# Two groups of a projection made together with seven block products for eight, and the groups' order changed

## The reference, cut to what matters

```python
z = rmsnorm(x, norm_g) @ w_in            # (256, 2048) @ (2048, 6144)
q_a, k_a, v_a, g_a, u_p, g_p, q_m, g_m = split(z)   # 1024 x4, 512 x4
y_a = causal_attention(q_a, k_a, v_a) * silu(g_a)   # 8 heads of 128, one block
y_p = windows_pool(u_p, w_pool, pool_scale) * silu(g_p)
mk, mv = split(rmsnorm(mem, mem_norm_g) @ w_mem_kv)  # 256 memory tokens
y_m = softmax(q_m @ mk.T) @ mv * silu(g_m)          # 4 heads of 128
out = rmsnorm(x + concat(y_a, y_p, y_m) @ w_out, final_norm_g)
```

## Time and profile before

| | |
|---|---|
| median of 3 runs | 434.19 us (433.77 to 434.23) |
| profiled execution | 435.72 us, span 433.9 us |
| TensorE busy | 424.4 us |
| VectorE busy | 285.3 us |
| ScalarE busy | 232.1 us |
| GpSimd busy | 36.0 us |
| read from HBM | 90.72 MB, 214 GB/s over the span |

### The profile page before, as it was taken

One profiled execution on the slowest core, in us unless ns is written; L12 is line 12 of the kernel. 1 busy time (PEld: TensorE's weight loads), 2 busy tenths in 40 slices (PEclk: granted clock), 3 DMA queues, 4 the chain that ended last, 5 costly groups with the idle time before them and its releaser, 6 DMA issues.

```text
span 433.9 us, 5989 instructions
## 1 busy us (share of the span) xinstructions
PE 424.4 (98%) x2256; PEld 364.9 (84%) x2256; DVE 285.3 (66%) x308; ACT 232.1 (53%) x314; POOL 36.0 (8%) x60
## 2 busy tenths in 40 slices
PE   9999999999999999999999999999999999999993
PEld 8888888878888888888888888888899888888882
DVE  4875764265484657646558686967677479897842
ACT  6764684284343434646554544555465566765621
POOL 1000000000100000000023140002000211000160
PEclk9999999999999999999999999999999999999998
DMA  8999969969856565443635655474745999567023
GB/s 283 401 402 412 406 203 351 115 223 124 313 186 201 174 211 168 148 144 97 210 106 170 203 186 193 152 237 147 239 150 187 252 403 256 210 233 284 18 84 111
DMA packets 27387, 93.20 MB, mean 215 GB/s; under 512 B 3680, under 2 KB 4192, under 8 KB 26464
## 3 DMA queue, kind: packets, MB, share of 16 engines
q1 hardware_dynamic: 24336, 82.21, 58.0%
q10 hardware_dynamic: 2448, 8.52, 5.1%
q0 software_dynamic: 576, 2.10, 2.8%
HBM read 90.72 MB, written 2.10 MB: 214 GB/s over the span
## 4 chain that ended last, share of the span: by engine, by line
PE 91%; DMA 3%; issue 2%; DVE 1%; ACT 0%; POOL 0%; DVEq 0%; POOLq 0%; ACTq 0%
PE ps L521 33%; PE ps L524 16%; PE ps L537 8%; PE ps L539 8%; PE ps L538 8%; DMA rstd_rows<-rstd_in 3%; PE ps L502 3%; PE ps L574 2%; PE ps L573 2%; PE ps L575 2%; PE ps L558 1%; PE ps L559 1%; PE ps L557 1%; PE ps L509 1%; PE ps L655 1%
## 5 line engine op out<-in xcount | busy, mean ns | idle before, releaser
L967 DVE TENSOR_TENSOR w_lo<-w_raw,w_hi 128x1024 fp32r<-128x1024 f32 x135 | 170.3, 1276 | 96.1 <-ACT w_hi L746 95.9
L521 PE MATMUL ps<-xT,w_hi 128*128 128x512 f32 x640 | 201.7, 396 | 1.0 <-DVE w_lo L967 1.0
L746 ACT ACTIVATE w_hi<-w_raw 128x1024 fp32r<-128x1024 f32 x135 | 141.0, 1057 | 109.7 <-PE ps L524 59.8
L524 PEld LDWEIGHTS ps<-xT,w_lo 128*128 128x128 f32 x640 | 120.2, 188 | 28.4
L524 PE MATMUL ps<-xT,w_lo 128*128 128x256 f32 x640 | 125.8, 278 | 0.0
L521 PEld LDWEIGHTS ps<-xT,w_hi 128*128 128x128 f32 x640 | 97.8, 189 | 1.4 <-DVE w_lo L967 1.2
L537 PE MATMUL ps<-w_hi,xT 128*128 128x512 f32 x64 | 25.3, 396 | 0.0
L539 PE MATMUL ps<-w_hi,xT 128*128 128x512 f32 x64 | 24.9, 390 | 0.0
L538 PE MATMUL ps<-w_lo,xT 128*128 128x512 f32 x64 | 24.9, 389 | 0.0
L847 ACT ACTIVATE part_b<-ps 128x1024 f32<-128x1024 f32 x11 | 11.3, 1028 | 19.8 <-PE ps L524 19.8
L537 PE MATMUL ps<-w_hi,yT 128*128 128x512 f32 x46 | 17.9, 389 | 0.0
(11 more groups left out here) (178 smaller groups left out, 539.1 us busy)
## 6 DMA issues: line engine op xcount, KB each, us to landing
w_raw<-in_w_in SPq DMA_DIRECT2D x96, 512.0 KB, 4.3
w_raw<-in_w_out SPq DMA_DIRECT2D x30, 512.0 KB, 5.1
w_raw<-in_w_mem_kv SPq DMA_DIRECT2D x13, 512.0 KB, 12.8
x_t_raw<-in_x_t SPq DMA_DIRECT2D x8, 256.0 KB, 13.5
rows<-in_x ACTq DMA_DIRECT2D x2, 1024.0 KB, 10.5
rows<-in_mem ACTq DMA_DIRECT2D x2, 1024.0 KB, 13.1
f<-in_w_out SPq DMA_DIRECT2D x4, 512.0 KB, 7.8
f<-in_w_out POOLq DMA_DIRECT2D x4, 512.0 KB, 9.4
```

Of the source, the lines that this page charges most:

```text
L521: pe.matmul(ps[:, bank0(g) + f, :], hi[:, t, f * P:(f + 1) * P], moving[:, kt], start=(kt == 0), stop=(kt == KT - 1), skip_group_check=True)
L524: m = pe.matmul(ps[:, bank0(g) + f, 0:S], lo[:, t, f * P:(f + 1) * P], moving[:, kt, 0], start=False, stop=(kt == KT - 1), skip_group_chec ...
L746: act.activation(halves_of(n)[0], whole_of(n), ACT.Copy).then_inc(hi_done, 1)
L967: dve.tensor_tensor(lo, whole_of(n), hi.bitcast(F32), ALU.subtract).then_inc(lo_done, 1)
```

## The change

V0 and V1 are made together as OUT1 and OUT2 are: 22 units, of which 14 are block products with 6 matmuls each, and 8 plain units. The sums of blocks of x are made by VectorE in K0 (`x_sum`) and split (`xs_hi`, `xs_lo`); the sums of weights come from a transfer that adds, on GpSimd's queue behind `mkT`, and from VectorE (`weight_sum`). ScalarE copies four finished products, scaled, into `v` and `gate`; `values_one` and `values_two` complete the values. U comes next, with job 0, then GA0 with job 1, GA1, GP. The squares of mem, its reciprocal root, its write and its read come two units later. The gate GA1 is now followed by GP.

```diff
-(MK, MV, Q0, Q1, K0, K1, V0, V1, GA0, GA1, U, GP, QM, GM, OUT0) = range(15)
+(MK, MV, Q0, Q1, K0, K1, V0, V1, U, GA0, GA1, GP, QM, GM, OUT0) = range(15)
...
+BLOCKS = 2
+
+
+def pair_units(one, two):
+    return ((N5, 0), (M2, 0), (N5, 1), (M2, 1), (one, 4), (M3, 0), (one, 5), (M1, 0), (M3, 1), (one, 6), (M1, 1),
+            (M6, 0), (one, 7), (M4, 0), (M4, 1), (M6, 1), (two, 4), (N7, 0), (two, 5), (two, 6), (N7, 1), (two, 7))
+
+
+def pair_loads(one, two):
+    return ((M2, 0), (M2, 1), (one, 4), (M3, 0), (one, 5), (M3, 1), (M6, 0), (M6, 1), (one, 6), (one, 7),
+            (two, 4), (two, 5), (two, 6), (two, 7))
...
+PAIRS = ((V0, V1), (OUT1, OUT2))
+V_UNITS, PAIR_UNITS = pair_units(V0, V1), pair_units(OUT1, OUT2)
+V_LOADS = pair_loads(V0, V1)
+LOADS = pair_loads(OUT1, OUT2) + tuple((LAST, a) for a in range(PPG))
+EXTRA = len(V_UNITS) - 2 * PPG
+FEWER = 2 * PPG - len(V_LOADS)
+V_PAIR = V0 * PPG
+V_END = V_PAIR + len(V_UNITS)
...
+SUM_STEPS = {V_PAIR - 2: (0, F6, 0), V_PAIR + 4: (0, F6, 1), V_PAIR + 6: (0, F7, 0), V_PAIR + 9: (0, F7, 1),
+             PAIR + 2: (1, F6, 0), PAIR + 4: (1, F6, 1), PAIR + 6: (1, F7, 0), PAIR + 9: (1, F7, 1)}
...
+X_SUM_STEPS = {K0 * PPG + 2: 0, K0 * PPG + 3: 1, K0 * PPG + 4: 2, K0 * PPG + 5: 3}
+BANK = {V0: 0, V1: 2, OUT0: 4, OUT1: 0, OUT2: 2, LAST: 4}
 TOKENS_ON_ROWS = (MV, V0, V1)
-CAUSAL_JOBS = {V1: 0, GA0: 1}
+CAUSAL_JOBS = {U: 0, GA0: 1}
 MEM_JOB = GM
-JOBS = (V1, GA0, GM)
+JOBS = (U, GA0, GM)
 FACTOR = {Q0: SCALE, Q1: SCALE, QM: SCALE, GA0: 0.5, GA1: 0.5, GP: 0.5, GM: 0.5}
-BRANCHES = (V1, GA0, GP, GM)
-SQUARE_STEPS = {16: (0,), 17: (1,), 18: (2,), 19: (3,), 24: (4,), 25: (5,), 26: (6,), 27: (7,)}
+BRANCHES = (U, GA0, GP, GM)
+SQUARE_STEPS = {16: (0,), 17: (1,), 18: (2,), 19: (3,), 26: (4,), 27: (5,), 28: (6,), 29: (7,)}
...
+X_MEAN, MEM_MEAN = 20, 32
+SPREAD_WRITE, SPREAD_READ = {22: 0, 34: 1}, {24: 0, 36: 1}
...
+                if a == 1:
+                    sp.wait_ge(x_lo, PPG)
+                    for i in range(BLOCKS):
+                        sp.dma_start(x_f4[:, i], in_dram[V1 - Q0, 2 * i]).then_inc(f4_landed[0][i], 16)
+                if a == 5:
+                    for i in range(BLOCKS):
+                        sp.dma_start(x_f567[:, i, 0], in_dram[V0 - Q0, 2 * i]).then_inc(f5_landed[0][i], 16)
+                sp.wait_ge(lo_done, K0 * PPG + a + 1)
+                load(K1 * PPG + a, in_dram, K1 - Q0, a)
+            for r, (g, a) in enumerate(V_LOADS):
+                if r < RAW:
+                    sp.wait_ge(lo_done, K1 * PPG + r + 1)
+                else:
+                    slot_free(0, *V_LOADS[r - RAW])
+                pair_load(0, V_PAIR + r, in_dram, Q0, g, a)
...
+            for k in range(BLOCKS):
+                pool.wait_ge(f4_landed[0][k], 16)
+                pool.dma_start(x_f4[:, k], in_dram[V0 - Q0, 2 * k], accum_op=ALU.add).then_inc(f4_summed[0][k], 16)
+            for k in range(BLOCKS):
+                pool.wait_ge(f5_landed[0][k], 16)
+                pool.dma_start(x_f567[:, k, 0], in_dram[V0 - Q0, 2 * k + 1], accum_op=ALU.add).then_inc(f5_summed[0][k], 16)
...
+                if g == GA0:
+                    pool.wait_ge(pv_done, 4)
+                    for buf in (u_pad, sum_a, sum_b):
+                        pool.memset(buf[:, :, 0:PAD], 0.0).then_inc(pads_zero, 1)
...
+            def unit_of_pair(n):
+
+                q = pair_of(n)
+                g, a = unit(n)
+                if n == BEGIN[q]:
+                    pe.wait_ge(s_split, q + 1)
+                if (g, a) == (M1, 0):
+                    pe.wait_ge(snapped, snaps_done(q, SNAPS[M2, 1]))
+                if (g, a) == (PAIRS[q][0], 4):
+                    pe.wait_ge(snapped, snaps_done(q, SNAPS[N5, 1]))
+                if (g, a) == (M4, 0):
+                    pe.wait_ge(snapped, snaps_done(q, SNAPS[M1, 1]))
+                if (g, a) == (PAIRS[q][1], 4):
+                    pe.wait_ge(snapped, snaps_done(q, SNAPS[M4, 1]))
+                pe.wait_ge(lo_done, n + 1)
+                (pair_piece if g < GROUPS else block_product)(n).then_inc(piece_used, 1)
...
+                if V_PAIR <= n < V_END:
+                    if unit(n) in SNAPS:
+                        bank = bank0(V0) if g == N5 else bank0(V1) + 1
+                        h = int(g in (N5, M4))
+                        dst = {M2: v[:, 0, COLS:], N5: v[:, 1, 0:COLS], M1: v[:, 0, 0:COLS],
+                               M4: gate[:, 0:TPP, :].rearrange("p f s -> p (f s)")}[g]
+                        act.wait_ge(piece_used, n + 1)
+                        act.activation(dst, ps[:, bank, :], ACT.Copy, scale=rstd_in[:, 0, h:h + 1]).then_inc(snapped, 1)
+                    for m in pieces_to_split(n):
+                        split_hi(m)
+                    continue
...
+                if n == K0 * PPG + 6:
+                    act.wait_ge(x_summed, 1)
+                    act.activation(xs_hi[:, :, :, :, :], s_raw[:, :, :, :, :], ACT.Copy).then_inc(s_hi_done, 1)
...
+            def x_sum(j):
+
+                def part(s, k, h):
+                    return xT[:, 0:BLOCKS * NF, k, h * P:(h + 1) * P].bitcast(F32).rearrange(
+                        "p (i s t) c -> p i s t c", i=BLOCKS, s=2)[:, :, s]
+
+                dst = s_raw[:, :, j]
+                low = gate[:, 0:NF, :].rearrange("p (i t) (a c) -> p i t a c", i=BLOCKS, a=2)[:, :, :, 0]
+                if j == 0 or j == 2:
+                    left, right = ((0, 1), (1, 1)) if j == 0 else ((0, 0), (0, 1))
+                    dve.tensor_tensor(low, part(left[0], 1, left[1]), part(right[0], 1, right[1]), ALU.subtract)
+                    settle(dve.tensor_tensor(dst, part(left[0], 0, left[1]), part(right[0], 0, right[1]), ALU.subtract))
+                    settle(dve.tensor_tensor(dst, dst, low, ALU.add))
+                else:
+                    before, s, op = (s_raw[:, :, 0], 0, ALU.subtract) if j == 1 else (s_raw[:, :, 1], 1, ALU.add)
+                    settle(dve.tensor_tensor(dst, before, part(s, 0, 0), op))
+                    m = dve.tensor_tensor(dst, dst, part(s, 1, 0), op)
+                    if j == 1:
+                        settle(m)
+                    else:
+                        m.then_inc(x_summed, 1)
+
+            def split_sums(lo, hi):
+
+                dve.tensor_tensor(lo[:, :, :, :, :], s_raw[:, :, :, :, :], hi[:, :, :, :, :].bitcast(F32),
+                                  ALU.subtract).then_inc(s_split, 1)
+
+            def values_one():
+
+                first = slice(0, COLS)
+                dve.wait_ge(rstd_ready, 1)
+                dve.wait_ge(snapped, snaps_done(0, SNAPS[M4, 1]))
+                settle(dve.tensor_tensor(v[:, 1, first], v[:, 1, first],
+                                         gate[:, 0:TPP, :].rearrange("p f s -> p (f s)"), ALU.subtract))
+                dve.wait_ge(piece_used, unit_in(0, M6, 1) + 1)
+                for h, op in ((0, ALU.subtract), (1, ALU.add)):
+                    m = dve.scalar_tensor_tensor(out=v[:, h, first], in0=ps[:, bank0(V0) + h, :], scalar=rstd_in[:, 0, h:h + 1],
+                                                 in1=v[:, h, first], op0=ALU.mult, op1=op)
+                m.then_inc(evacuated, 1)
...
+            def values_two():
+
+                second = slice(COLS, 2 * COLS)
+                dve.wait_ge(piece_used, V_END)
+                dve.scalar_tensor_tensor(out=v[:, 0, second], in0=ps[:, bank0(V1), :], scalar=rstd_in[:, 0, 0:1],
+                                         in1=v[:, 0, second], op0=ALU.mult, op1=ALU.add)
+                dve.tensor_scalar(v[:, 1, second], ps[:, bank0(V1) + 1, :], rstd_in[:, 0, 1:2], None, ALU.mult
+                                  ).then_inc(evacuated, 1)
...
-                if g in TOKENS_ON_ROWS:
-                    dst = {V0: v[:, :, 0:COLS], V1: v[:, :, COLS:]}[g]
-                    dve.wait_ge(rstd_ready, 1)
-                    for h in range(TH):
-                        m = dve.tensor_scalar(dst[:, h], ps[:, bank0(g) + h, :], rstd_in[:, 0, h:h + 1], None, ALU.mult)
-                    m.then_inc(evacuated, 1)
-                    return
...
+                if g == U:
+                    m.then_inc(evacuated, 1)
+                    dve.wait_ge(evacuated, U + 1)
+                    dve.wait_ge(rstd_spread[0], 16)
+                    dve.tensor_tensor(dst[:, :, :], dst[:, :, :], x_rstd[:, :, :].to_broadcast([P, NF, S]), ALU.mult
+                                      ).then_inc(u_ready, 1)
+                    return
...
+                    for m in pieces_to_split(n):
+                        split_lo(m)
+                    if n in SUM_STEPS:
+                        weight_sum(*SUM_STEPS[n])
+                    if n == V_PAIR + 16:
+                        values_one()
+                    if n == V_END - 1:
+                        values_two()
+                    continue
...
-                if g == V0 and a == 4:
+                if g == GA1 and a == 5:
...
```

(47 more changed lines are left out.)

191 lines of the change are left out of this document (99 added, 92 removed).

## The result

The changed kernel takes 441.28 us (median of 6 runs, 439.81 to 443.7) against 434.08 (6 runs, 433.75 to 434.23): ratio 1.0171, interval 1.0138 to 1.0203. It is slower by 7.2 us. The sign was forecast, the size was not: 438.6 is 2.7 too low, and the time is 0.1 above the range's upper end of 441.2. Its runs also spread over 3.9 us where those of before spread over 0.5.

What follows compares the result with a forecast made beforehand. TensorE's list was taken to bound the kernel, busy 424.4 of 433.9 us. Terms -2.3 + 0.6 + 0.9 + 1.1 + 0.6 + 3.5 = +4.4 us gave 438.6 us, range 435.2 to 441.2.

Steps and rivals of the forecast that it cites:

- gain of the seven products: V0 and V1 made as a pair: 180 matmuls on TensorE instead of 192, saving 2.3 us.
- K0 and K1: x_sum, later reciprocal roots and VectorE's lock with GpSimd delay unit 43's w_lo: +0.6 us, between 0 and 3.
- start of the pair: After K1's end, unit 51's w_lo stands behind kT, wanted at 145.8 and coming at 146.67: +0.9 us.
- job 0 in U: Scores after U's first unit wait for V1's values, which stand behind a split: +1.1 us.
- job 1's turning in GA0: U's evacuation on VectorE delays the mask, so the second pair of probabilities comes late: +0.6 us.
- GP: GA1's gate falls into GP with the pool windows; unit 5's w_lo 2.2 us late, unit 7's 1.2: +3.5 us.
- Hidden: Work costing no time: extra splits, four sums, product copies, 3 MB more of weights, mv moved to GA1.
- Rival B: First sum late through adding transfers issued after mkT, delaying unit 51: 440.6 us, up to 442; chance 0.13.
- A fall of the clock behind a hole: Lower granted clock after TensorE's holes would make the forecast wrong; the earlier 0.97 us hole brought none.
- The shift from the profiled execution to the median, -1.5: Profiled execution forecast at 440.1 us; median of runs taken 1.5 lower, giving 438.6.
- C: Rival: one split more of lead on VectorE everywhere, holes summing to less than 2.3 us: 433.0 us; chance 0.10.
- D: Rival: block products slow or held, gain under 0.5 us, holes partly cancelled: within 0.2% either way; chance 0.07.

Runs made afterwards that it cites:

- all edits but one: Changed kernel with five moves, one part taken back at a time: job 0's values 432.59 us, windows 435.13, first sum and K1's evacuation 435.71.
- all edits: Changed kernel with first sum later, K1's evacuation inside the pair, values_two before the split, U's scaling in GA0, pool windows spread: 431.79 us.
- the windows moved: Changed kernel with pool windows spread over GA1 and GP's first step, mv's scaling moved to GA0: 437.77 us, ratio 1.0089.
- the first sum out of the way: Changed kernel with the first weight sum three units later, in the pair's second unit: 437.52 us, ratio 1.0083.
- squares edit: Kernel before the change, with only mem's squares, mean, write and read two units later: 434.00 us, ratio 1.0000.
- the start's part: Kernel with all five moves, but first sum and K1's evacuation back as in the changed kernel: 435.71 us, ratio 1.0032.
- GP's part: Kernel with all five moves, but pool windows whole in GP's first step and mv's scaling in GA1 again: 435.13 us, ratio 1.0034.
- the trace without a hole at the start: Changed kernel with first sum later and K1's evacuation behind the splits of the pair's third unit: 437.23 us, ratio 1.0078.

## Why the forecast was right in sign and too small

Costs read from the runs with all edits but one, beside the terms of the prediction:

| step | forecast | measured |
|---|---|---|
| gain of the seven products | -2.3 | -2.2 (434.0 to 431.8, all edits) |
| K0 and K1 | +0.6 | no hole in any trace |
| start of the pair | +0.9 | +3.9 (holes of 1.98 to 3.24, partly with a fall of the clock) |
| job 0 in U | +1.1 | +0.8 (hole 0.95) |
| job 1's turning in GA0 | +0.6 | hole 0.37, +0.6 between two traces, not run alone |
| GP | +3.5 | +3.3 (holes 2.02 and 0.78) |
| sum | +4.4 | -2.2 + 3.9 + 0.8 + 0.6 + 3.3 = +6.4; the kernel itself +7.2 |

The cost of the turning is read from the first turning of job 0 to the pool's matmuls: 80.75 us in the trace with the windows moved (203.94 to 284.69), where this hole is the only one, and 80.18 with all edits (197.79 to 277.97).

**The step that failed is "Start of the pair: +0.9 us"**, with the line under "Hidden" that counted "3 MB more of weights" as nothing. The mechanism was walked rightly from K1's end on (0.73 with the first sum out of the way, 0.9 forecast). What I left out stands ahead of it in the same queue: the first sum, two units before the pair, and its second operand. I had asked when the adding transfers land that it needs; they were in time (ScalarE's copy of the first piece, at 131.75, waited only for TensorE). I had not asked what these transfers do to SP's plain loads behind them, among which is M6's raw piece. It is this wait, 1.7 to 3.0 us on VectorE, that makes 0.9 into 2.0 to 3.2, and a fall of the clock in most runs does the rest of the +3.9. Rival B had its place (unit 51) and gave 440.6, the number nearest to the result, but by another cause: it made the first `x_f` piece late, and that piece, unit 48's, was copied at 131.75 and split at 132.84 without waiting for its transfer.

**A fall of the clock behind a hole was not in the sum.** I named it as what would make the forecast wrong, and gave as evidence that 0.97 us brought none. That was too little: the holes forecast were over 2 us, and no row of before showed so long a one in mid-kernel. By their clocks, the median runs of the start's part and of GP's part hold one such fall each, so +3.9 and +3.3 contain it. What remains between +6.4 and +7.2, 0.8 us, is not assigned to a part.

**The shift from the profiled execution to the median, -1.5, does not hold for the changed kernel.** The forecast of the median does not rest on it, as 434.19 + 4.4 gives the same 438.6; the 440.1 for the profiled execution does. I read the profiled execution of before as 1.5 above its median and took the same for after. The squares edit showed a trace of the same median whose span is 1.6 shorter, so before's profile was an untypical one; after's own profiled execution, 439.85, lies 1.4 below its median. The forecast for the profiled execution, 440.1, fits 439.85 by luck, because errors cancel. K1 ends at 139.91, 1.7 ahead of the 141.60 of before and not 0.6 behind it: the K0 term and the hole of the earlier trace rows are missing, and TensorE's first product came 0.4 earlier. That is -2.3. From there to the end the kernel takes 298.1 us where before took 292.3, 5.8 more and not 3.8: the start's hole (2.40 for 0.9) and the clock (1.7) against GP (2.03 for 3.5) make most of these +2.0.

**K0.** The write of the reciprocal roots took 10.8 us (103.88 to 114.64), 10 forecast. But the read behind it landed in 5.0 us and not 8.3, so GpSimd's `mkT` came at 119.81 and was nearly over (122.2) when K0's `kT` began at 121.75. That `kT` took its usual 1.23, so the lock I feared cost VectorE nothing here. The timeline of GpSimd, which answers to the earlier trace rows:

```profile
119.81 2.41 POOL L537 TENSOR_TENSOR mkT<-mkT,mem_rstd 128x1024 f32<-128x1024 f32 x1 [18.13 <-DMA mem_rstd<-rstd_rows]
```

**GP went as walked**, in order and nearly in size. The timeline of VectorE, which answers to the earlier trace rows:

```profile
266.93 1.22 DVE L1216 SCALAR_TENSOR_TENSOR gate<-ps,part_b 128x1024 f32<-128x1024 f32 x1 [1.58 <-ACT part_b L975]
...
271.56 2.59 DVE L1098 TENSOR_TENSOR w_lo<-w_raw,w_hi 128x1024 fp32r<-128x1024 f32 x1 [0.94 <-ACT w_hi L863]
274.07 1.21 DVE L1285 TENSOR_TENSOR sum_a<-u_pad 128x1024 f32<-128x1024 f32 x1
...
280.47 1.22 DVE L1098 TENSOR_TENSOR w_lo<-w_raw,w_hi 128x1024 fp32r<-128x1024 f32 x1
281.60 1.22 DVE L1365 SCALAR_TENSOR_TENSOR gate<-part_b,gate 128x1024 f32<-128x1024 f32 x1
```

The split beside GpSimd's product takes 2.59 us, the windows start 7.14 behind the evacuation (forecast 7.15), and GP's late split follows them. The hole is 2.03 for 2.2. The second one was 0.8 for 1.2. Counted from start to start the two cost 3.3, which is the forecast less 0.2: from job 0's turning to the first output product it is 142.93 us with the windows alone back (197.46 to 340.39) and 139.59 with all edits (197.79 to 337.38).

**Job 0 and job 1** stand where they were put, 0.95 for 1.1 and 0.37 for 0.6. From K1's end to job 0's scores the trace without a hole at the start has 45.14 us and the one with all edits 44.03, so this hole cost its 1.1. Rivals C and D are out: C's hidden holes all show but K0's, and the products gain 2.2, not under 0.5.

## What to carry to other kernels

When a new operation goes into a strict queue, walk what stands behind it, and for each operand ask which transfer brings it and what else is in flight then: here a sum that costs nothing held a split for 2 us because of a load that four adding transfers had slowed from 4.2 to 10.7 us. A saving of TensorE time is real only once every split is in time; the same 12 matmuls fewer gave +7.2 us with the moved work where the splits had to wait for it and -2.2 with the same work put in other steps. A hole of 2 us on TensorE can also cost a fall of the clock behind it. Before a forecast is shifted from a profiled execution to the median, look whether that execution has a hole that the others need not have.
